# A hybrid decoder step on one core: the prompt's attention issued by head pair instead of by head group

## The chip, the core and the metric

The kernel runs on one core of a Trainium2 chip. A core has TensorE (PE, with its weight loads shown apart as PEld), VectorE (DVE), ScalarE (ACT), GpSimd (POOL) and SyncE (SP, which here only issues DMAs). Each takes its instructions in the order in which they are written; semaphores tie the engines together. The metric is the device time of one execution in microseconds, as the median of the runs shown.

## What is computed

The reference is one inference step of a two-layer model for a prompt of 1024 tokens and 8 sample sequences of 4 tokens. Layer one joins native sparse attention (8 query heads, 2 key heads, head size 64) with a gated MLP, layer two is a gated linear recurrence. The change touches the prompt's attention alone. For each block of 128 queries it has three branches, each a softmax with its own keys, merged by gates:

```python
p_c = jax.nn.softmax(jnp.where(ok_c, s_c, NEG), axis=-1) * ok_c
o_c = jnp.einsum('bghtn,bngd->btghd', p_c.astype(vc.dtype), vc)
...
p_s = jax.nn.softmax(s_s.reshape(B, NSA_KV_HEADS, HPG, Tb, n_key), axis=-1)
o_s = jnp.einsum('bghtk,bgtkd->btghd', p_s.astype(v_s.dtype), ...)
...
p_w = jax.nn.softmax(jnp.where(ok_w, s_w, NEG), axis=-1)
o_w = jnp.einsum('bghtk,bkgd->btghd', p_w.astype(vw.dtype), vw)
...
o = (g[:, :, 0] * oc + g[:, :, 1] * osl + g[:, :, 2] * ow)
y_nsa = o * jax.nn.silu(z_nsa)
```

Branch c attends to compressed blocks of 64 keys, s to selected blocks (with 16 blocks of 64 in the prompt all that lie behind the query are selected), w to a sliding window of 512. Everything is float32.

## The kernel before

The prompt has eight tiles of 128 queries. In tile i the compressed branch has 2i + 2 columns for all heads at once; the selected branch has (i + 1) x 128 key columns; the window branch as many, at most 640. A head pair c (0 to 3) is the heads c and c + 4, one of each key head. So a tile has nine "pairs": one c, four s, four w (PAIRS). A group is the four s pairs or the four w pairs of a tile (GROUPS), a unit a chunk of at most 512 score columns of one pair (UNITS).

One pair goes through five steps. PE multiplies queries and keys into a PSUM bank pair (scores; line 1192 is the helper of all matmuls). DVE adds the position bias, writes the sum to the buffer `probs` and keeps the row's minimum (L1758). ACT takes the exponential in place and the row sum (L1051). POOL takes the reciprocal of the sum with a power (L942) and multiplies sum and gate into the probabilities, in place, one instruction a head (L948). PE then turns each 128 x 128 block of probabilities (a flip, line 1196) into a PSUM bank, ACT (L1059) or DVE (L1774) copies the bank to the buffer `pT`, and PE multiplies with the values into bank 7, where the 4 x 128 columns are the four pairs and the two halves of the partitions the two key heads. At a tile's end DVE multiplies bank 7 by the gate path (`y`, L1778). The c pair has its own small form (L930 to L938 on POOL, `c_turn`, `c_values`).

`attention_steps` writes down one order of steps; PE and DVE each walk through it, ACT through the order that `act_order` makes of it, POOL through PAIRS. A step of kind `turn` (j, b, g) is for key block b of group j and key head g: four flips, one of each pair, fill one bank. It waits for the scaling of the group's last pair:

```python
pe.wait_ge(norm_done, last_pair(j) + 1)
```

The `values` step of a key block has two instructions of 512 columns, one for each key head, all four pairs side by side, in the two column halves of the array. Key head 0 is copied by ACT, key head 1 by DVE. The next group's scores are spread over the key blocks of the present one, so scores are one group ahead, and `probs` has one set for s and one for w. Three banks (4, 5, 6) take turned blocks, `pT` has two buffers. SP starts the sample sequences' cache loads for its first half when the selected group of tile 7 has been turned, those of the second half (twelve transfers of 256 KB each time) when the last y is done.

Of the kernel before, what the change touches and what calls it, by code (L numbers as in the profile page):

```python
# [23 lines left out]
P = 128  # L24
# [88 lines left out]
GROUPS = [(kind, i) for i in range(PT) for kind in "sw"]  # L113
# [3 lines left out]
LAST_UNIT = [max(n for n, u in enumerate(UNITS) if u[0] == e) for e in range(len(PAIRS))]  # L117


def last_pair(j):  # L120

    return 9 * (j // 2) + 4 * (j % 2) + 4


def blocks(j):
    return key_cols(*GROUPS[j])[0] // P


FEW = 2


def attention_steps():

    steps = []
    issued = 0

# [9 lines left out]
    def group_end(j):  # L146
        return LAST_UNIT[last_pair(j)] + 1

    score(group_end(0))
    late = None  # L150

    def values():
        j, b = late
        steps.append(("values", late))
        if GROUPS[j][0] == "w" and b == blocks(j) - 1:
            steps.append(("y", GROUPS[j][1]))

    for j, (kind, i) in enumerate(GROUPS):
        nk = blocks(j)
        ahead = group_end(j + 1) if j + 1 < len(GROUPS) else issued  # L160
        if kind == "s":
            steps.append(("c_turn", i))
        for b in range(nk):
            steps.append(("turn", (j, b, 0)))
            if late and b == 0 and kind == "s":
                values()
                late = None
            steps.append(("turn", (j, b, 1)))
            left = ahead - issued
            score(issued + -(-left // max(1, nk - 1 - b)) if left > 0 else issued)  # L170
            if b == nk - 1 and j + 2 < len(GROUPS) and blocks(j + 1) <= FEW:
                score(group_end(j + 2))
            if kind == "s" and b == 0:
                steps.append(("c_values", i))
            if late:
                values()
            late = (j, b)
    values()
    return steps


def act_order(steps):

    order, pending = [], []
    for x in steps:
        if x[0] == "scores":
            pending.append(x)
            continue
        need = -1
        if x[0] == "turn":  # L190
            need = LAST_UNIT[last_pair(x[1][0])]
        elif x[0] == "c_turn":
            need = LAST_UNIT[9 * x[1]]
        while pending and pending[0][1] <= need:
            order.append(pending.pop(0))
        order.append(x)
        if x[0] == "turn":
            order += pending
            pending = []
    return order + pending  # L200


def bank_uses(steps):

    return {x: k for k, x in enumerate(x for x in steps if x[0] in ("c_turn", "turn"))}

# [15 lines left out]
def build(nc, ins, outs):  # L222
    ctx = ExitStack()
    with ctx:
# [66 lines left out]
        probs = {"s": view(region_w, 8448, HEADS, SEQ), "w": view(region_w, 16640, HEADS, WCOLS)}  # L291
        bias_far = view(region_w, 21760, HEADS, P)
        pT = [view(region_w, 22784 + 1024 * j, KVH, 512) for j in range(2)]
# [248 lines left out]
        bank_use = bank_uses(steps)  # L542

        block_order = [x[1][:2] for x in steps if x[0] == "turn" and x[1][2] == 0]
        nth_block = {x: f for f, x in enumerate(block_order)}
        dve_uses = [x for x in steps if x[0] == "c_turn" or x[0] == "turn" and x[1][2] == 1]
        nth_dve = {x: n for n, x in enumerate(dve_uses)}
        by_bank = list(bank_use)

        def bank_is_free(eng, k):  # L550

            if k >= 3:
                x = by_bank[k - 3]
                if x in nth_dve:
                    eng.wait_ge(dve_turned, nth_dve[x] + 1)
# [1490 lines left out]
```

## Time and profile before

| | us |
|---|---|
| median of 3 runs (lowest, highest) | 1247.98 (1246.66, 1253.84) |
| the profiled execution | 1246.11 |
| its span, first to last instruction | 1244.3 |
| PE busy in the span | 1101.1 (88%) |
| DVE busy | 508.3 (41%) |
| ACT busy | 369.7 (30%) |
| POOL busy | 291.7 (23%) |

The prompt's attention begins at about 395 us, after the input projections, and its last y ends at 734.9; the sample sequences, the output projection and the second layer follow. Busy time of matmuls is modelled, since they are pipelined: prices are better read as the distance from one row's start to the next row's start. PE's clock is granted at one of two levels, 1.2 and 2.4 GHz, shown as 0.50 and 1.00.

### The profile page before, as it was taken

Reading aid. Unit: us, or ns where it says so; the run is one execution under the profiler, and the core shown is the slowest. Engines: PE = TensorE matmul, PEld = TensorE weight load, DVE = VectorE, ACT = ScalarE, POOL = GpSimd, SP = SyncE. Lnnn points to the kernel's source line nnn. Section 1 sums busy time; section 2 is a strip of 40 time slices with the busy share of each in tenths; the row PEclk is TensorE's granted clock in tenths of the full one; section 3 lists DMA queues with packets and bytes.
Section 4 is the critical chain, followed back from the end, with each engine's and each line's share of the span. In section 5 each row is a group of like instructions: output and inputs, shape, how many; then the busy total and the mean of one; then the engine's idle time right before and its main releaser. Section 6 shows DMA issues by size and latency. Waiting matters only on the chain.

```text
span 1244.3 us, 14223 instructions
## 1 busy us (share of the span) xinstructions
PE 1101.1 (88%) x5553; PEld 822.5 (66%) x5553; DVE 508.3 (41%) x1048; ACT 369.7 (30%) x632; POOL 291.7 (23%) x395
## 2 busy tenths in 40 slices
PE   5999999999997675877888876899999999998997
PEld 3555547999997343434444444688688888997884
DVE  1222213111232343454555523544469996315222
ACT  1011103111111333344354410322237777114111
POOL 1223317320001656355354400000101221000110
PEclk9999999999998677788898886799999999998999
DMA  9110034232103100000000056222231110601221
GB/s 311 35 43 26 16 75 115 75 92 51 41 11 96 41 1 1 1 1 1 1 1 1 1 177 162 83 87 89 68 90 35 34 35 18 203 1 56 68 102 59
DMA packets 70448, 74.69 MB, mean 60 GB/s; under 512 B 21730, under 2 KB 55570, under 8 KB 70383
## 3 DMA queue, kind: packets, MB, share of 16 engines
q1 hardware_dynamic: 65260, 69.15, 17.8%
q0 software_dynamic: 2496, 3.04, 0.8%
q10 hardware_dynamic: 2626, 1.62, 0.5%
q8 instruction: 44, 0.72, 0.2%
q14 instruction: 22, 0.17, 0.0%
HBM read 62.16 MB, written 16.34 MB: 63 GB/s over the span
## 4 chain that ended last, share of the span: by engine, by line
PE 81%; POOL 6%; ACT 4%; DVE 2%; issue 2%; DMA 2%; SPq 1%; ACTq 0%; POOLq 0%; DVEq 0%
PE ps L1192 74%; PE ps L1196 7%; POOL region_w L948 4%; POOL inv L942 2%; ACT region_w L1051 1%; DMA region_y<-in_w_in_a 1%; ACT L1135 1%; ACT region_w L1135 1%; ACT region_w L1059 1%; DMA region_w<-in_cache_win 1%; POOL inv L930 1%; DVE region_w L1758 0%; DMA region_w<-rel_rows_dram 0%; SPq L722 0%; SPq L724 0%
## 5 line engine op out<-in xcount | busy, mean ns | idle before, releaser
L1196 PE MATMUL ps<-ident,region_w 128*128 128x128 f32 (+2 forms) x738 | 116.6, 305 | 87.4 <-POOL region_w L948 66.6
L1196 PEld LDWEIGHTS ps<-ident,region_w 128*128 128x128 f32 (+2 forms) x738 | 92.1, 156 | 153.2 <-issue 114.4
L1192 PE MATMUL ps<-h1T_hi,w_c_hl 128*128 128x352 f32 x768 | 151.1, 326 | 12.9 <-ACT region_w L1135 8.7
L1192 PE MATMUL ps<-hT_hi,w_fm_hl 128*128 128x352 f32 x768 | 146.5, 324 | 2.8 <-DVE w_fm_hl L1629 2.8
L1192 PEld LDWEIGHTS ps<-h1T_hi,w_c_hl 128*128 128x128 f32 x768 | 129.0, 190 | 17.7 <-ACT region_w L1135 13.1
L1192 PEld LDWEIGHTS ps<-hT_hi,w_fm_hl 128*128 128x128 f32 x768 | 127.7, 188 | 3.0 <-DVE w_fm_hl L1629 2.9
L829 POOL TENSOR_SCALAR ms<-ss 128x1 f32<-128x1 f32 (+1 forms) x27 | 12.6, 468 | 386.4 <-ACT region_w L1185 177.3
L1192 PE MATMUL ps<-region_y,region_w 128*128 128x512 f32 (+3 forms) x288 | 100.4, 507 | 0.0
L948 POOL TENSOR_SCALAR region_w<-region_w,inv,gates 128x640 f32<-128x640 f32 (+7 forms) x128 | 98.7, 781 | 6.7
L1192 PE MATMUL ps<-region_w 128*128 128x512 f32 (+4 forms) x308 | 98.9, 514 | 1.4 <-DVE region_w L1816 1.4
L1059 ACT COPY region_w<-ps 128x512 f32<-128x512 f32 x66 | 38.6, 585 | 199.0 <-PE ps L1196 199.0
L1051 ACT ACTIVATE region_w<-region_w,negm 128x640 f32<-128x640 f32 (+7 forms) x128 | 92.6, 727 | 2.6 <-DVE negm L1758 2.5
L1192 PE MATMUL ps<-region_q 64*128 64x512 f32 (+3 forms) x384 | 87.6, 571 | 5.9 <-DVE negm L1758 2.4
L1192 PE MATMUL ps<-h1T_lo,w_c_hl 128*128 128x352 f32 x384 | 85.9, 325 | 0.0
L1192 PE MATMUL ps<-w_outa_hi,ya_hl 128*128 128x512 f32 (+1 forms) x288 | 81.3, 400 | 4.6 <-DVE w_outa_lo L1872 4.6
L1192 PE MATMUL ps<-hT_lo,w_fm_hl 128*128 128x352 f32 x384 | 82.7, 323 | 0.0
L1192 PEld LDWEIGHTS ps<-region_y,region_w 128*128 128x128 f32 (+1 forms) x288 | 52.8, 186 | 44.5 <-issue 37.5
L1192 PE MATMUL ps<-region_w,region_q 128*64 128x512 f32 x264 | 81.1, 698 | 1.2 <-DVE region_w L1774 1.2
L1192 PEld LDWEIGHTS ps<-region_w 128*128 128x128 f32 (+2 forms) x308 | 47.6, 181 | 43.6 <-issue 32.2
L1774 DVE COPY region_w<-ps 128x512 f32<-128x512 f32 x66 | 45.5, 690 | 73.2 <-PE ps L1196 72.8
L942 POOL TENSOR_TENSOR inv<-sums,minus_one 128x2 f32<-128x2 f32 x64 | 45.2, 706 | 95.0 <-ACT region_w L1051 95.0
L1192 PEld LDWEIGHTS ps<-h1T_lo,w_c_hl 128*128 128x128 f32 x384 | 66.1, 189 | 0.0
(243 smaller groups left out, 1488.5 us busy)
## 6 DMA issues: line engine op xcount, KB each, us to landing
region_w<-in_x_prompt SPq DMA_DIRECT2D x16, 512.0 KB, 3.5
region_w<-in_w_in_c SPq DMA_DIRECT2D x16, 512.0 KB, 3.9
rel_rows_dram<-rel_once_dram SPq DMA_DIRECT2D x8, 576.0 KB, 5.5
region_w<-in_w_in_a SPq DMA_DIRECT2D x16, 256.0 KB, 3.6
region_w<-in_w_in_a SPq DMA_DIRECT2D x8, 512.0 KB, 3.7
region_w<-in_cache_nsa SPq DMA_DIRECT2D x16, 256.0 KB, 3.0
x_dram<-region_w SPq DMA_DIRECT2D x8, 512.0 KB, 2.6
region_w<-in_w_out_c SPq DMA_DIRECT2D x2, 2048.0 KB, 9.9
```

What stands on the lines that cost most here:

```text
L829: pool.tensor_scalar(ms[0:r, norm, i:i + 1], ss[0:r, norm, i:i + 1], 1.0 / D, EPS, ALU.mult, ALU.add).then_inc(pool_chain, 1)
L930: pool.tensor_tensor(inv[:, 0, :], sums[:, i % 2, 0, :], minus_one[:, 0:HEADS], ALU.pow).then_inc(pool_chain, 1)
L942: pool.tensor_tensor(inv[:, b, c::HPG], sums[:, i % 2, b, c::HPG], minus_one[:, 0:KVH], ALU.pow).then_inc(pool_chain, 1)
L948: m = pool.tensor_scalar(x, x, inv[:, b, h:h + 1], gates[:, i, b * HEADS + h:b * HEADS + h + 1], ALU.mult, ALU.mult)
L1051: m = nc.scalar.activation(buf, buf, ACT.Exp, bias=negm[:, at:at + 1], scale=-1.0, accum_out=sums[:, i % 2, b, h:h + 1])
L1059: nc.scalar.copy(pT[f % 2][:, 0, :], ps[:, 4 + k % 3, :]).then_inc(act_turned, 1)
L1135: nc.scalar.activation(r_buf.rearrange("p (a b) -> p a b", a=3), bank3(n), ACT.Sigmoid, bias=vecT[:, VEC["b_rg_a"] + c:VEC["b_rg_a"] + c + ...
L1192: return nc.tensor.matmul(out, l, r, start=start, stop=stop, skip_group_check=True)
L1196: return nc.tensor.transpose(out, x, ident[0:k, 0:k])
L1774: v.tensor_copy(pT[f % 2][:, 1, :], ps[:, 4 + k % 3, :]).then_inc(dve_turned, 1)
```

## The change

The order is written by head pair. A `turn` step is now (e, b): pair e, key blocks b and b + 1 (one if there is no second), both key heads: four or two flips in one bank. It waits for that pair's scaling alone. Its `values` step has, for each of the blocks and key heads, an instruction of 128 columns, and stands behind the second turn that follows (one is kept back in `late` when the next is issued). Scores run up to five pairs ahead (`ahead`). The probabilities lie in six buffers of one pair each, taken in rotation (`probs_slot`); DVE waits, before it writes a buffer, for the last turn of the pair that had it. `pT` has four buffers of two blocks. A turn of even index b / 2 is copied by ACT, the others by DVE. The first instruction that clears bank 7 is now a selected one; the wait for the tile before's y stands there; `c_values` comes later, in the stream. Line numbers after the attention's helpers move up by some lines: flips are L1185, matmuls L1181, ACT's copies L1047, DVE's L1772.

```diff
+P_RING = 6
+PT_RING = 4
+TURN_BANKS = 3
...
+def probs_slot(e):
+
+    return (e - e // 9 - 1 + 2) % P_RING
...
+    def ahead(e):
+        return LAST_UNIT[min(e + P_RING - 1, len(PAIRS) - 1)] + 1
+
+    score(ahead(0))
+    for e, (kind, i, c) in enumerate(PAIRS):
+        if kind == "c":
+            continue
+        firsts = list(range(0, blocks(e), 2))
+        for at, b in enumerate(firsts):
+            steps.append(("turn", (e, b)))
+            left = max(0, ahead(e) - issued)
+            score(issued + -(-left // (len(firsts) - at)))
+            values(1)
+            late.append(("values", (e, b)))
+        if kind == "s" and c == 1:
             steps.append(("c_turn", i))
...
+            values(1)
+            late.append(("c_values", i))
+    values(0)
     return steps
+
+
+def on_act(x):
+
+    return x[0] == "turn" and x[1][1] // 2 % 2 == 0
...
-                    sp.wait_ge(turned, bank_use["turn", (len(GROUPS) - 2, PT - 1, 1)] + 1)
+                    sp.wait_ge(turned, last_turn[len(PAIRS) - 1 - HPG] + 1)
...
-                    pe.wait_ge(norm_done, last_pair(j) + 1)
-                    for c in range(HPG):
-                        m = flip(ps[:, 4 + k % 3, c * P:(c + 1) * P],
-                                 probs[kind][:, g * HPG + c, b * P:(b + 1) * P])
+                    e, b = n
+                    pe.wait_ge(norm_done, e + 1)
+                    for j in range(min(2, blocks(e) - b)):
+                        for g in range(KVH):
+                            m = flip(ps[:, 4 + k % TURN_BANKS, (2 * j + g) * P:(2 * j + g + 1) * P],
+                                     probs[probs_slot(e)][:, g, (b + j) * P:(b + j + 1) * P])
                     m.then_inc(turned, 1)
...
-                    for g in range(KVH):
-                        gp = slice(g * HD, (g + 1) * HD)
-                        m = mm(ps[gp, 7, :], (v_s if kind == "s" else v_w)[:, first // P + b, gp],
-                               pT[f % 2][:, g, :], False, kind == "w" and b == blocks(j) - 1)
+                    turn_out(pe, k)
+                    if kind == "s" and c == 0 and b == 0 and i >= 1:
+                        pe.wait_ge(y_nsa, i)
+                    for j in range(min(2, blocks(e) - b)):
+                        for g in range(KVH):
+                            gp = slice(g * HD, (g + 1) * HD)
+                            m = mm(ps[gp, 7, c * P:(c + 1) * P],
+                                   (v_s if kind == "s" else v_w)[:, first // P + b + j, gp],
+                                   pT[k % PT_RING][:, j, g, :], kind == "s" and c == 0 and b + j == 0,
+                                   kind == "w" and c == HPG - 1 and b + j == blocks(e) - 1)
                     m.then_inc(values_done, 1)
...
+                    was = [x for x in last_turn if x < e and probs_slot(x) == probs_slot(e)]
+                    if a == 0 and was:
+                        dve.wait_ge(turned, last_turn[max(was)] + 1)
```

PE before, from the end of tile 6's window group into tile 7's selected group. Flips read `ident,region_w`, values write `64x512`, scores are the `region_q` rows, `ident,lc` and `vc_bd` belong to the compressed branch.

```order
L1192 MATMUL ps<-region_w,region_q 64x512 x2
L1196 MATMUL ps<-ident,region_w 128x128 x8
L1192 MATMUL ps<-region_w,region_q 64x512 x2
L1196 MATMUL ps<-ident,lc 128x128
L1196 MATMUL ps<-ident,region_w 128x128 x4
L1192 MATMUL ps<-region_w,region_q 64x512 x2
L1196 MATMUL ps<-ident,region_w 128x128 x4
L1192 MATMUL ps<-region_q 128x128 x2
L1192 MATMUL ps<-region_q 128x512 x2
L1192 MATMUL ps<-region_w,vc_bd 128x128 x4
L1196 MATMUL ps<-ident,region_w 128x128 x8
```

The four flips behind `ident,lc` wait for the whole selected group's scaling; all its scores stand ahead of these rows. PE after, at the same place: the first row is the values of tile 6's last window turn, the flips are all of tile 7's first selected pairs:

```order
L1181 MATMUL ps<-region_w,region_q 64x128 x2
L1185 MATMUL ps<-ident,region_w 128x128 x4
L1181 MATMUL ps<-region_q 128x128 x2
L1181 MATMUL ps<-region_w,region_q 64x128 x4
L1185 MATMUL ps<-ident,region_w 128x128 x4
L1181 MATMUL ps<-region_q 128x512 x2
L1181 MATMUL ps<-region_w,region_q 64x128 x4
L1185 MATMUL ps<-ident,region_w 128x128 x4
L1181 MATMUL ps<-region_q 128x128 x2
L1181 MATMUL ps<-region_w,region_q 64x128 x4
```

Flips, scores and values now alternate in short runs, and the stream has no step at which a whole group is waited for.

ACT before, over the scores of tile 7's selected pairs (1024 columns; two instructions a pair), which it takes while tile 6's window group is turned:

```order
L1044 ACTIVATE lc<-lc 128x128
L1051 ACTIVATE region_w,sums<-region_w,negm 128x1024 x2
L1059 COPY region_w<-ps 128x512
L1051 ACTIVATE region_w,sums<-region_w,negm 128x1024 x2
L1059 COPY region_w<-ps 128x512
L1051 ACTIVATE region_w,sums<-region_w,negm 128x1024 x2
```

ACT after, over the same scores:

```order
L1032 ACTIVATE lc<-lc 128x128
L1047 COPY region_w<-ps 128x512 x2
L1047 COPY region_w<-ps 128x256
L1039 ACTIVATE region_w,sums<-region_w,negm 128x1024 x2
L1047 COPY region_w<-ps 128x512
L1047 COPY region_w<-ps 128x256
L1039 ACTIVATE region_w,sums<-region_w,negm 128x1024 x2
```

A pair's exponentials now stand behind both of ACT's copies of the pair that is being turned; before, one copy of each key block stood between them. POOL's and SP's instructions stand in the same order as before.

## Rows read from the trace of the kernel before

**Rows 1.** Stretch: us; busy PE, PEld, DVE, ACT, POOL; PEclk, DMA share, GB/s.

```profile
395.00:735.00 340.00, 263.58 (x1313) 136.60 (x1313) 158.44 (x529) 132.34 (x330) 159.93 (x216) 0.82 0.07 22
```

**Rows 2.** Waits from 395 to 735: engine, line, waited for; us, times, longest.

```profile
POOL inv L942 <- ACT region_w L1051: 95.0, 29, 10.8
...
PE ps L1196 <- POOL region_w L948: 66.6, 14, 7.1
```

**Rows 3.** PE over time at a group's end: start, us, what, idle before.

```profile
692.55 1.09 PE L1196 MATMUL ps<-ident,region_w 128*128 128x128 f32 x4 [4.59 <-POOL region_w L948]
693.57 1.98 PE L1192 MATMUL ps<-region_w,region_q 128*64 128x512 f32 x4
695.47 1.12 PE L1196 MATMUL ps<-ident,region_w 128*128 128x128 f32 x4
```

**Rows 4.** PE over time inside a window group of tile 6.

```profile
642.85 0.66 PE L1196 MATMUL ps<-ident,region_w 128*128 128x128 f32 x4
643.44 1.35 PE L1192 MATMUL ps<-region_q 64*128 64x128 f32 x8
644.72 1.16 PE L1192 MATMUL ps<-region_w,vc_bd 128*128 128x128 f32 x8
645.71 1.04 PE L1196 MATMUL ps<-ident,region_w 128*128 128x128 f32 x8
...
652.45 1.13 PE L1192 MATMUL ps<-region_q 64*128 64x512 f32 x4
653.51 1.08 PE L1192 MATMUL ps<-region_w,region_q 128*64 128x512 f32 x4
654.52 1.09 PE L1196 MATMUL ps<-ident,region_w 128*128 128x128 f32 x8
655.54 0.49 PE L1192 MATMUL ps<-region_q 64*128 64x128 f32 x4
655.96 1.08 PE L1192 MATMUL ps<-region_w,region_q 128*64 128x512 f32 x4
```

**Rows 5.** Weight loads over time, of c_values and of 512-column values.

```profile
595.65 0.97 PEld L1192 LDWEIGHTS ps<-region_w,vc_bd 128*128 128x128 f32 x8 [0.95 <-issue]
...
598.90 0.20 PEld L1192 LDWEIGHTS ps<-region_w,region_q 128*64 128x64 f32 x4 [0.76 <-issue]
```

**Rows 6.** POOL: two pairs of tile 0 over time; groups by line (busy, mean ns).

```profile
403.93 0.71 POOL L942 TENSOR_TENSOR inv<-sums,minus_one 128x2 f32<-128x2 f32 x1
405.58 0.71 POOL L942 TENSOR_TENSOR inv<-sums,minus_one 128x2 f32<-128x2 f32 x1
L948 POOL TENSOR_SCALAR region_w<-region_w,inv,gates 128x640 f32<-128x640 f32 x40 | 34.6, 874 | 2.1
L930 POOL TENSOR_TENSOR inv<-sums,minus_one 128x8 f32<-128x8 f32 x8 | 13.2, 1651 | 74.6 <-DVE sums L1763 74.6
```

**Rows 7.** Busy time by stretch, for the granted clock (PEclk, after the busy times).

```profile
409.00:421.00 12.00, 11.63 (x54) 8.49 (x55) 4.81 (x29) 3.77 (x17) 6.23 (x12) 0.50 0.01 2
421.00:428.00 7.00, 5.12 (x33) 2.56 (x32) 5.03 (x26) 4.65 (x18) 4.62 (x8) 1.00 0.00 1
725.00:735.00 10.00, 9.21 (x55) 4.48 (x53) 3.46 (x5) 2.34 (x4) 0.00 (x0) 1.00 0.61 192
```

**Rows 8.** Groups by line: copies and exponentials; busy, mean ns; idle before, releaser.

```profile
L1774 DVE COPY region_w<-ps 128x512 f32<-128x512 f32 x66 | 45.5, 690 | 73.2 <-PE ps L1196 72.8
L1059 ACT COPY region_w<-ps 128x512 f32<-128x512 f32 x66 | 38.6, 585 | 199.0 <-PE ps L1196 199.0
L1051 ACT ACTIVATE region_w<-region_w,negm 128x640 f32<-128x640 f32 x40 | 32.8, 822 | 0.8 <-DVE negm L1758 0.8
```

**Rows 9.** SP's sample loads and PE's first use of the second half.

```profile
718.00 8.50 SPq L724 DMA_DIRECT2D region_w<-in_cache_nsa  x8
735.64 8.00 SPq L724 DMA_DIRECT2D region_w<-in_cache_nsa  x8
752.61 1.97 PE L1196 MATMUL ps<-ident,region_w 128*128 128x128 f32 x8 [8.38 <-DMA region_w<-in_cache_win]
```

More of the change, by code:

```diff
@@ L135, in attention_steps @@
     issued = 0
+    late = []
     def score(upto):
@@ L144, in score, with values @@
         issued = max(issued, upto)
[L146 to L161, printed above, removed]
-            steps.append(("c_turn", i))
[L163 to L178, printed above, removed]
-    return steps
+    def values(keep):
+        while len(late) > keep:
+            x = late.pop(0)
+            steps.append(x)
+            if x[0] == "values":
+                e, b = x[1]
+                if PAIRS[e][0] == "w" and PAIRS[e][2] == HPG - 1 and b + 2 >= blocks(e):
+                    steps.append(("y", PAIRS[e][1]))
+    def ahead(e):
[12 more added lines that the diff above has]
+        if kind == "s" and c == 1:
+            steps.append(("c_turn", i))
+            values(1)
+            late.append(("c_values", i))
+    values(0)
+    return steps
+def on_act(x):
+    return x[0] == "turn" and x[1][1] // 2 % 2 == 0
 def act_order(steps):
@@ L188, in act_order @@
             continue
[L189 to L193, printed above, removed]
+        if x[0] not in ("turn", "c_turn"):
+            continue
+        need = LAST_UNIT[x[1][0] if x[0] == "turn" else 9 * x[1]]
         while pending and pending[0][1] <= need:
             order.append(pending.pop(0))
[L196 to L199, printed above, removed]
+        if on_act(x):
+            order.append(x)
+        order += pending
+        pending = []
     return order + pending
-def bank_uses(steps):
-    return {x: k for k, x in enumerate(x for x in steps if x[0] in ("c_turn", "turn"))}
 FM_A = ([("z", j, "act") for j in range(4)]
@@ L289, in build @@
         bias = view(region_w, 0, HEADS, SEQ)
-        probs = {"s": view(region_w, 8448, HEADS, SEQ), "w": view(region_w, 16640, HEADS, WCOLS)}
+        probs = [view(region_w, 8448 + KVH * SEQ * j, KVH, SEQ) for j in range(P_RING)]
         bias_far = view(region_w, 21760, HEADS, P)
-        pT = [view(region_w, 22784 + 1024 * j, KVH, 512) for j in range(2)]
+        pT = [view(region_w, 22784 + 512 * j, 2, KVH, P) for j in range(PT_RING)]
         probT_c = view(region_w, 24832, P)
@@ L541, in build, with turn_out @@
         steps = attention_steps()
[L542 to L555, printed above, removed]
-                else:
-                    eng.wait_ge(act_turned, nth_block[x[1][:2]] + 1)
+        turns = [x for x in steps if x[0] in ("turn", "c_turn")]
+        nth_turn = {x: k for k, x in enumerate(turns)}
+        last_turn = {x[1][0]: k for k, x in enumerate(turns) if x[0] == "turn"}
+        act_count = [sum(on_act(y) for y in turns[:k + 1]) for k in range(len(turns))]
+        def turn_out(eng, k):
+            if on_act(turns[k]):
+                eng.wait_ge(act_turned, act_count[k])
+            else:
+                eng.wait_ge(dve_turned, k + 1 - act_count[k])
         def spread(ap, n, axis=2):
@@ L1321, in _ @@
             for what, n in steps:
-                k = bank_use.get((what, n))
-                if k is not None:
-                    bank_is_free(pe, k)
+                k = nth_turn.get((what, n))
+                if k is not None and k >= TURN_BANKS:
+                    turn_out(pe, k - TURN_BANKS)
                 if what == "scores":
```

73 lines of the change are left out of this document (35 added, 38 removed).

## The prediction

> **What bounds the kernel now.** I read the busy time by stretch first. The prompt's attention runs from 395 to 735 us, 340 us, and in it TensorE (PE) is busy 264 us at a mean granted clock of 0.82, GpSimd (POOL) 160, VectorE (DVE) 158, ScalarE (ACT) 132 [rows 1]. So PE is the nearest bound, and still it idles 76 us and runs part of the rest at the lower clock. The waits say why: 66.6 us of PE's idle time, in 14 waits, ends with POOL's scaling of probabilities (L948), and POOL itself idles 95.0 us behind ACT's exponentials [rows 2]. A group is four head pairs, and PE turns nothing of a group before POOL has scaled its last pair, while scores run only one group ahead. So at each group's end the last chunk of scores goes through DVE, ACT and POOL with PE idle. The row at 692.55 is such a place: PE waited 4.59 us for L948 [rows 3]. The first work after it is slow: 512-column values (four records) took 1.90 us from 693.57 to 695.47 [rows 3], and 1.01 from 653.51 to 654.52 [rows 4].
>
> **PE's prices at the full clock**, from start to next start [rows 4]: a run of 4 flips 0.59 (642.85 to 643.44), of 8 flips 1.02 (654.52 to 655.54), so 0.11 a flip and 0.37 for 2. Scores: a 512-column unit 1.06 (from 652.45), a 128-column unit alone 0.42 (from 655.54), one of each in one run 1.28 (from 643.44). So 128 more columns in a run cost 0.22, and what is left of the lone unit, 0.20, is the price of changing over to scores. A 512 unit then streams 0.86, and on that line 256 columns stream 0.43 and 384 0.65. Values of 512 columns cost 1.01, that is 0.86 and a change of 0.15.
>
> **Before, by these prices.** 66 key blocks x (1.02 + 1.01) = 134. Score units (44 of 512, 12 of 384, 12 of 256, 28 of 128) stream 37.8 + 7.8 + 5.2 + 6.2 = 57, and 49 runs x 0.20 = 10. The compressed branch I take as 2.2 a tile in both kernels (0.99 of it from 644.72 to 645.71 [rows 4]), 18. Sum 218. The other 122 us of the stage are waits and the lower clock. That is what there is to win.
>
> **The change part by part.**
> Flips: 528 in both, but now in 152 runs (112 of 4, 40 of 2): 112 x 0.59 + 40 x 0.37 = 81, where 66 x 1.02 = 67 stood.
> Values: 66 pairs of 512-column instructions become 264 pairs of 128-column ones. The trace before has none of that shape. Below, a pair can't cost less than a quarter of the old stream, 0.22; above, it could cost what a lone 128-column score pair does, 0.42. I take 0.22 and one change of 0.15 a run, 0.59 for two blocks and 0.37 for one, since the nearest row, c_values (four 128-column instructions, eight records), takes 0.99 in all. So 112 x 0.59 + 40 x 0.37 = 81, where 67 stood; at 0.42 for each pair it would be 111, 30 more.
> Scores: the same 57, but 89 runs, so 18 of changes and not 10. The compressed branch stays 18. Sum 81 + 81 + 75 + 18 = 255: **PE gets 37 us more of its own work.**
> What goes is the group's end. A pair is turned as soon as its own scaling is done, and scores run five pairs ahead. POOL's pair takes 1.65 us at 128 columns (403.93 to 405.58) and, with 0.87 for each of its two L948 rows at 640, 2.5 [rows 6]. PE needs for such a pair 2 x (0.59 + 0.59) + 2 x 0.37 + 0.42 + 1.06 = 4.6. So POOL is hidden from the third tile on, by 2 us a pair. In tiles 0 and 1 POOL sets the pace: 8 x 1.65 + 8 x 1.86 (256 columns, on the line) + 2 x 2.35 for the compressed pairs (1.65 of it L930 [rows 6]) = 33, where PE's own is 28 (pairs of 0.37 + 0.37 + 0.42 = 1.16 and 0.59 + 0.59 + 0.63 = 1.81): +5. Before the first pair is scaled (404) PE can only score: of these 9 us about 3.5 are used, for one compressed pair and five of 0.4 to 0.5, so +5.5.
> Evictions: 132 of 512 columns become 152 of 512 or 256. ACT takes 96 (38.6 us of busy time become about 50), DVE 56 (45.5 become about 34). So ACT's work in the stage becomes about 143, DVE's 147, POOL's stays 160 [rows 1], all well under PE's 255: they lie beside it. In a 640-column pair ACT has 2 x 0.82 + 0.585 + at most 0.585 = 2.8 us [rows 8] of PE's 4.6. A run's eviction begins about 0.7 us after the run's start and takes 0.6 to 0.7, so the values could start 1.5 us after it. In the order they stand behind the second run that follows, with two other runs of values between: 5 x 0.59 = 3 us or more. That covers an exponential pair of ACT (1.7) that the copy has to wait for, nearly. I book +3 for what is missed, with 0 and 45 as ends.
> Waits: that for y moves to the first values of a tile; behind it on PE stand the next flips, and for those wait ACT and DVE. DVE reaches y up to one unit of logits late (two passes of 512 columns, by the copy's 0.69 [rows 8] 1.4) and takes about 0.7, PE has 0.6 to 1.6 of other work: 0 to 2 us at seven tiles, +5. DVE's new wait for a buffer is for the pair six before, whose last turn stands ahead of these scores on PE: 0.
> SP's wait for the last group's turns becomes one for the last selected pair: same place. POOL's order is unchanged.
>
> **The clock.** The row 409 to 421 shows 0.50 with PE busy 11.63 of 12 us; from 421 it is 1.00 [rows 7]. The new kernel starts at the lower level too. Its first tile is sparse, and twice as dear it is still near POOL's pace; tile 1 at that level would add (1.8 x 1.81 - 1.86) x 8 = 11 us. I book +8, ends 0 and 20. Later no wait of several us is left.
>
> **Sum.** 255 + 5.5 + 5 + 8 + 5 + 3 = 281.5, and about 1 for the last y, against the stage's 340: -57.5. The tail: the sample's first twelve transfers, issued at 718.00, were due after 17 us as the second twelve were (735.64 to 752.61 [rows 9]), just as the last window group ended. Now four window pairs without scores follow the issue, 4 x 3.1 = 12.4 and y, about 14: up to 3 us of these transfers stick out and push the second twelve, +1.5. Together -56. The profiled execution's 1246.11 us (span 1244.3) become 1190; the median of the runs is 1.9 higher, so **1192 us**.
>
> **Rivals.**
> *Evictions come late* (0.3 us at each of 152 runs, three banks and four buffers not being enough): 46 in place of 3, 1235. For it: ACT takes its order as it stands, and a copy can stand behind an exponential pair that waits for DVE. Against: ACT and DVE idle 200 and 73 us at these copies for want of work [rows 8].
> *Weight loads stand in front of the short matmuls.* Four loads of 64 columns show 0.20 [rows 5]; 264 such sets in full are 53, about 45 over what the changes hold: 1237. Against: in c_values eight loads of 128 columns are busy 0.97 us [rows 5] of the 0.99 that the eight matmuls take, so they overlap. The Trainium skill, "TensorE: Matmul & The Clock Gate", Part 3, "What overlaps and what doesn't", says that weight loads overlap matmuls in flight only where the row group differs, which is not so here. With its load of P/1.2 ns, 53 ns for 64 columns, 528 loads would be 28 us, an estimate from that page, and the sum 1220; the c_values row speaks against it.
> *PE stays at the lower clock* (slower). Values cost 1.90 and 4 flips 1.02 there (692.55 to 693.57 [rows 3]), about 1.8 times as much. All 255 us so would be 204 more, less the 8 booked: 1388. The change loses once about 80 us of PE's work, a third, runs at that level (64 / 0.8). For it: runs get shorter, with more changes between. Against: from 725 to 735, where flips and values alternate with waits for evictions, the clock is 1.00 [rows 7]. The Trainium skill, same page, Part 4 (PE-mode transpose), says that the full rate does not engage for transposes; by that rule, with a third of PE's work in flips, this rival would be likelier. The row last named, half flips, speaks against it.
> *The run-ahead doesn't reach over a tile's start*: the compressed pair, its reciprocal of 1.65 us and y hold PE there as the groups' ends did, 8 x 3.5 = 28: 1220.
>
> **Chances.** Forecast with its own range 1174 to 1215: 0.72. Late evictions 0.10, loads 0.06, tile starts 0.05, lower clock 0.07. Low end: nothing for the clock, y, late evictions and the tail, -73.5 us and so 1174. High end: loads, 1237. A measurement here tells 0.5% (6 us) from no change. Faster: 0.72 + 0.05 and nearly all of the 0.16, 0.90; same 0.03; slower 0.07.
>
> **What would show it.** Right: no wait of PE for L948 over 2 us after 440; granted clock 1.00 from about 440 to the stage's end; flips and values about 81 us each at full clock, c_values' pace in the values; PE busy over 90% from tile 2 on; the stage's end near 680. Wrong: waits of PE for the copies (L1047, L1772) that sum to tens of us; values pairs at 0.4; 0.5 in the clock row past 450; idle PE at each tile's start behind y.

## The result and the profile after

The changed kernel takes 1185.09 us (median of 4 runs, 1181.83 to 1187.05) where the kernel before, run beside it, takes 1250.91 (4 runs): a ratio of 0.947, with an interval of 0.943 to 0.952. Forecast were 1192 (1174 to 1237). The profiled execution takes 1187.05 us (span 1185.2), 59.1 less than the one of before; the medians are 65.8 apart, since the profiled execution is the longest of the four here, and the one before was shorter than the four it is measured against. Three stretches account for the 59.1:

| us | before | after | difference |
|---|---|---|---|
| attention, from 395 to the end of the last y | 339.9 | 275.5 | -64.4 |
| sample stage, from there to the output projection's first matmul | 52.2 | 58.0 | +5.8 |
| the rest behind it | 459.0 | 458.5 | -0.5 |

So the attention gave 7 us more than forecast (282.5 us, the prediction's 281.5 and 1 for the last y), and in this execution the stage behind it took nearly 6 back.

Busy time of the changed kernel by stretch (us; PE, PEld, DVE, ACT, POOL; granted clock; DMA share; GB/s), to be read against [rows 1]:

```profile
395.00:671.00 276.00, 260.36 (x2104) 159.45 (x2104) 148.54 (x520) 143.86 (x360) 161.08 (x216) 0.96 0.09 28
430.00:672.00 242.00, 235.80 (x1972) 143.44 (x1971) 137.30 (x450) 129.61 (x301) 138.66 (x177) 1.00 0.05 14
476.00:670.00 194.00, 191.96 (x1626) 117.50 (x1625) 112.72 (x365) 99.04 (x215) 102.64 (x122) 1.00 0.06 16
```

PE is busy almost as long as before, though it now does more work, because hardly any of that work runs at 0.50. From the fourth tile on (third line) it is busy 99% of the time.

Its waits from 395 to 671 (us, times, longest), against [rows 2]:

```profile
POOL inv L929 <- ACT region_w L1039: 53.6, 30, 4.8
...
PEld ps L1181 <- ACT region_w L1047: 17.9, 27, 1.0
...
PE ps L1185 <- POOL region_w L936: 8.6, 4, 2.9
...
PE ps L1181 <- DVE region_y L1777: 2.6, 3, 0.9
```

The 66.6 us behind POOL are 8.6, and all but 1.2 of these lie before 430. No wait of PE's matmuls ends with a copy: the 17.9 us stand at the weight loads (PEld), which run ahead of the matmuls. PE in tile 5, as [rows 4] showed tile 6, then a tile's start with its wait for y, then the weight loads of the first rows:

```profile
560.56 0.66 PE L1185 MATMUL ps<-ident,region_w 128*128 128x128 f32 x4
561.15 0.66 PE L1181 MATMUL ps<-region_w,region_q 128*64 128x128 f32 x8
561.74 0.66 PE L1185 MATMUL ps<-ident,region_w 128*128 128x128 f32 x4
...
587.30 0.49 PE L1181 MATMUL ps<-region_q 64*128 64x128 f32 x4
588.64 0.66 PE L1181 MATMUL ps<-region_w,region_q 128*64 128x128 f32 x8 [0.85 <-DVE region_y L1777]
```

```profile
560.56 0.42 PEld L1185 LDWEIGHTS ps<-ident,region_w 128*128 128x128 f32 x4 [0.17 <-issue]
561.15 0.42 PEld L1181 LDWEIGHTS ps<-region_w,region_q 128*64 128x64 f32 x8 [0.17 <-issue]
```

From start to start four flips cost 0.59 us and the values of two blocks 0.59, the two prices of the forecast to the digit. The eight loads of a values run (two records for each instruction) are busy 0.42 us inside these 0.59.

And the stage behind the attention, against [rows 9]: SP's sample loads, PE's first work on each half, the first matmul of the output projection, and a stretch of that stage.

```profile
657.03 8.51 SPq L711 DMA_DIRECT2D region_w<-in_cache_nsa  x8
...
671.22 8.70 SPq L711 DMA_DIRECT2D region_w<-in_cache_nsa  x8
```

```profile
672.41 3.56 PE L1185 MATMUL ps<-ident,region_w 128*128 128x128 f32 x16 [2.66 <-DMA region_w<-in_cache_win]
...
687.68 1.97 PE L1185 MATMUL ps<-ident,region_w 128*128 128x128 f32 x8 [5.01 <-DMA region_w<-in_cache_win]
...
694.79 6.83 PE L1181 MATMUL ps<-avg,region_w 128*128 128x2 f32 x32
...
728.50 1.19 PE L1181 MATMUL ps<-w_outa_hi,ya_hl 128*128 128x512 f32 x2 [4.58 <-DVE w_outa_lo L1871]
```

```profile
679.00:734.00 55.00, 38.65 (x213) 28.88 (x214) 22.96 (x81) 11.96 (x22) 0.00 (x0) 0.50 0.47 135
...
691.00:711.00 20.00, 20.00 (x123) 15.69 (x122) 5.83 (x27) 1.44 (x6) 0.00 (x0) 0.50 0.52 149
```

The second half's first flips come 17.2 us behind the last y (17.7 before), so the transfers are not later. From there to the output projection are 40.8 us, and 34.5 before. The clock is 0.50 from 679 to 734 without a break, where the kernel before had two stretches at 1.00 (10.2 us together).

### The profile page after: what moved, and what is told of

It reads as the page before. It is cut to its first block, busy times and chain, and to the rows that moved or that the text cites. A ratio compares the mean times of both kernels' runs of the same rounds, so it can differ in the third digit from the quotient of the medians.

```text
span 1185.2 us, 15810 instructions
## 1 busy us (share of the span) xinstructions
PE 1106.7 (93%) x6345; PEld 854.2 (72%) x6345; DVE 497.2 (42%) x1038; ACT 381.2 (32%) x662; POOL 287.5 (24%) x395
## 4 chain that ended last, share of the span: by engine, by line
PE 88%; ACT 3%; DVE 2%; DMA 2%; issue 2%; POOL 1%; SPq 1%; ACTq 0%; DVEq 0%; POOLq 0%
PE ps L1181 79%; PE ps L1185 9%; DMA region_y<-in_w_in_a 1%; ACT L1124 1%; ACT region_w L1124 1%; DMA region_w<-in_cache_win 1%; POOL inv L917 0%; POOL region_w L936 0%; DVE region_w L1754 0%; SPq L711 0%; DMA region_w<-rel_rows_dram 0%; SPq L709 0%; ACT region_w L1114 0%; ACT w_c_hl L1067 0%; POOL inv L929 0%
## 5 line engine op out<-in xcount | busy, mean ns | idle before, releaser
L1181 PE MATMUL ps<-h1T_hi,w_c_hl 128*128 128x352 f32 x768 | 151.2, 326 | 12.8 <-ACT region_w L1124 8.7
L1185 PE MATMUL ps<-ident,region_w 128*128 128x128 f32 (+2 forms) x738 | 128.7, 301 | 27.9 <-POOL region_w L936 8.6
L1181 PE MATMUL ps<-hT_hi,w_fm_hl 128*128 128x352 f32 x768 | 147.7, 326 | 2.8 <-DVE w_fm_hl L1622 2.8
L1181 PEld LDWEIGHTS ps<-h1T_hi,w_c_hl 128*128 128x128 f32 x768 | 129.0, 190 | 17.7 <-ACT region_w L1124 13.1
L1185 PEld LDWEIGHTS ps<-ident,region_w 128*128 128x128 f32 (+2 forms) x738 | 86.4, 151 | 62.0 <-issue 31.3
L1181 PEld LDWEIGHTS ps<-hT_hi,w_fm_hl 128*128 128x128 f32 x768 | 128.9, 190 | 3.0 <-DVE w_fm_hl L1622 2.9
L1181 PE MATMUL ps<-region_w 128*128 128x512 f32 (+4 forms) x308 | 98.9, 514 | 1.4 <-DVE region_w L1815 1.4
L1181 PE MATMUL ps<-region_y,region_w 128*128 128x512 f32 (+3 forms) x288 | 99.1, 503 | 0.0
L1181 PEld LDWEIGHTS ps<-region_w,region_q 128*64 128x64 f32 x1056 | 55.1, 137 | 57.0 <-issue 32.4
L1181 PE MATMUL ps<-region_w,region_q 128*64 128x128 f32 x1056 | 91.8, 289 | 2.7 <-DVE region_y L1777 2.6
L1754 DVE CUSTOM_DVE_ANT_0 region_w<-ps,region_w 128x128 f32<-128x128 f32 (+3 forms) x128 | 57.7, 488 | 77.0 <-PE ps L1181 76.7
L1181 PE MATMUL ps<-region_q 64*128 64x512 f32 (+3 forms) x384 | 84.9, 526 | 2.1 <-DVE lc L1735 1.9
L1181 PE MATMUL ps<-h1T_lo,w_c_hl 128*128 128x352 f32 x384 | 85.8, 325 | 0.0
L1181 PE MATMUL ps<-w_outa_hi,ya_hl 128*128 128x512 f32 (+1 forms) x288 | 81.0, 399 | 4.6 <-DVE w_outa_lo L1871 4.6
L1181 PEld LDWEIGHTS ps<-region_y,region_w 128*128 128x128 f32 (+1 forms) x288 | 52.3, 184 | 43.8 <-issue 36.8
L1047 ACT COPY region_w<-ps 128x512 f32<-128x512 f32 (+1 forms) x96 | 49.7, 518 | 105.6 <-PE ps L1185 105.4
L1181 PE MATMUL ps<-hT_lo,w_fm_hl 128*128 128x352 f32 x384 | 83.1, 325 | 0.0
L1181 PEld LDWEIGHTS ps<-region_w 128*128 128x128 f32 (+2 forms) x308 | 47.6, 181 | 43.6 <-issue 32.2
L1181 PEld LDWEIGHTS ps<-h1T_lo,w_c_hl 128*128 128x128 f32 x384 | 66.2, 189 | 0.0
```

What stands on the lines that cost most here:

```text
L1047: nc.scalar.copy(pT[k % PT_RING][:, 0:w, :, :].rearrange("p b g t -> p (b g t)"), ps[:, 4 + k % TURN_BANKS, 0:w * KVH * P]).then_inc(act_t ...
L1181: return nc.tensor.matmul(out, l, r, start=start, stop=stop, skip_group_check=True)
L1185: return nc.tensor.transpose(out, x, ident[0:k, 0:k])
L1754: x = v.tensor_tensor_reduce(probs[probs_slot(e)][:, g, a:b], ps[:, slot + g, 0:b - a], table, 1.0, least, ALU.add, ALU.min, to)
```

## The experiments

Theory: in the kernel before, PE waited at each group's end for the chain through DVE, ACT and POOL, and ran slowly behind the wait; the wait for one pair and the scores five pairs ahead remove both, for about 37 us of added work at known prices. Rivals: only the finer wait or only the run-ahead matters; copies come late; a change between runs costs other than reckoned; the clock is a consequence that costs nothing by itself. Medians stand beside those of the kernel before on the same chip (1247 to 1253), and the ratio is to these. In profiled executions the attention's first matmul lies between 395 and 399, so stages are compared from there.

### The whole group is waited for again

```diff
-        need = LAST_UNIT[x[1][0] if x[0] == "turn" else 9 * x[1]]
+        need = LAST_UNIT[x[1][0] + HPG - 1 - PAIRS[x[1][0]][2] if x[0] == "turn" else 9 * x[1]]
...
-                    pe.wait_ge(norm_done, e + 1)
+                    pe.wait_ge(norm_done, e + HPG - PAIRS[e][2])
```

> The changed kernel with one part undone: a turn waits again until the last pair of its group of four is scaled, and ACT takes the group's exponentials ahead of the group's first copy; the six buffers, the scores five pairs ahead, the 128-column values and the turns of two blocks stay. Theory (the grain of the wait and the run-ahead work together): for a selected group the scores of the fourth pair are issued only in the last turns of the tile before, so PE waits 4 to 6 us for POOL's scaling at each of 7 tile starts and 0 to 2 us at the window groups, and the granted clock falls again after some of these waits: +45 us (30 to 60), 1230 us. Rival A (the run-ahead alone hides the chain, the grain of the wait is nothing): +0 to 10 us, at most 1195. Rival B (the grain is all): as the kernel before, near 1250.

Measured: 1245.04 us, 0.999 (0.997 to 1.001). All of the gain is gone with one wait (and ACT's order that goes with it), though the ring of six buffers, the run-ahead and the short values stay. Waits of the stage, and PE at a tile's start:

```profile
PE ps L1185 <- POOL region_w L936: 50.3, 11, 7.8
```

```profile
458.41 0.66 PE L1181 MATMUL ps<-region_w,region_q 128*64 128x128 f32 x8
466.51 1.09 PE L1185 MATMUL ps<-ident,region_w 128*128 128x128 f32 x4 [7.44 <-POOL region_w L936]
```

The clock's mean over the stage falls from 0.96 to 0.87. Rival A is out. The theory's size was too low (+45, at most +60, where the medians give +60 and the ratios +64), and by its time alone this run fits rival B, the grain is all, as well. The next two runs decide that: there the fine wait stays. The 37 us of added work stay in here too, so the run doesn't say that the run-ahead is worth nothing by itself.

### Scores two and three pairs ahead

```diff
-P_RING = 6
+P_RING = 3
...
```

With four buffers it is `P_RING = 4`.

> The changed kernel with three buffers of probabilities in place of six, so scores run two pairs ahead and not five (the compressed sums stand one unit earlier on DVE, so that the order has no cycle); the wait for one pair alone stays. Theory (the chain through DVE, ACT and POOL takes 6 to 7 us for a pair of 512 columns or more, and the run-ahead hides it): a pair's scores now stand one pair of PE's work (4 to 6 us) ahead, or none for the first two selected pairs of a tile, so PE waits for POOL 1 to 2 us at most pairs and about 5 us at two pairs of each tile, with the lower clock behind them: +100 us (60 to 140), about 1285, slower than the kernel before. Rival (the finer wait is the gain, the ring only needs to be there): +0 to 15 us, at most 1200.

> The changed kernel with four buffers of probabilities, scores three pairs ahead in place of five. Theory (the chain needs 6 to 7 us, two pairs of PE's work are 8 to 12 in the later tiles; only the third selected pair of a tile, whose scores are held up by the compressed pair's place in the count, has one pair of work): waits of 2 to 3 us at 7 tile starts and about 10 us more in the first three tiles: +25 us (10 to 40), about 1210. Rival (three ahead are enough): within 5 us. Rival (the dependence on the ring is steep, as from two to five): over +50.

Measured: 1283.32 us with three buffers, 1.030 (1.028 to 1.031), and 1213.79 with four, 0.974 (0.970 to 0.977). PE's waits for POOL with three:

```profile
PE ps L1185 <- POOL region_w L936: 74.1, 32, 6.0
```

and with four:

```profile
PE ps L1185 <- POOL region_w L936: 28.1, 13, 5.2
```

With five, three and two pairs of run-ahead PE waits 8.6, 28.1 and 74.1 us for POOL. The sizes are the theory's (1285 and 1210 were expected). With two pairs, less than the one group (four pairs) of the kernel before, the fine wait is slower than that kernel; with three it brings about half of the gain. So rival B is out: the fine wait needs the run-ahead. Not run was the other way round, the old order with its long values and waits for a group, but with scores more than one group ahead; whether that would do as well is open.

### Values one turn earlier

```diff
-            values(1)
+            values(0)
```

> The changed kernel with values one turn earlier: none is kept back, each run of values stands behind the first turn that follows its own. From a turn's start to its values are then three runs of 0.59 us, 1.8 us, and a copy ends about 1.4 us after its turn's start, later where ACT is in a pair of exponentials (1.7 us). Theory (copies are on time with two turns between, and only just with one): +10 us (0 to 20) in waits of PE for the copies of L1047. Rival (late evictions were already there in the changed kernel, hidden in the rows as a slower pace): +25 to 45 us. Rival (the holding back does nothing): within 3 us.

Measured: 1188.62 us, 0.953 (0.951 to 0.954), an interval that overlaps the changed kernel's; the stage is 280 us in place of 276. One wait of PE ends with a copy:

```profile
PE ps L1181 <- DVE region_w L1772: 2.1, 1, 2.1
```

The rest is a lower mean clock in the stage (0.94 for 0.96), so the copies were on time but for one, and the turn held back is worth some 4 us in this execution. The rival of late evictions is out.

### Turns of one key block

```diff
-        firsts = list(range(0, blocks(e), 2))
+        firsts = list(range(0, blocks(e), 1))
...
```

The widths of flips, copies and values follow, and ACT and DVE still copy by turns.

> The changed kernel with turns of one key block: 264 runs of 2 flips and 264 runs of 2 values instructions in place of 152 runs each; columns, ring and waits stay. Theory (prices: a change over to another kind of run costs 0.15 us on top of 0.11 a flip and 0.22 a pair of 128-column values): flips 264 x 0.37 = 98 in place of 81, values 98 in place of 81, a few more changes to scores: +35 us (30 to 42), about 1220, with PE busy all the same. Rival (a change costs nothing, a run's cost is in its columns): +0 to 5 us. Rival (the fixed part of 264 copies makes evictions late): +50 us or more, in waits of PE for L1047 and the DVE copies.

Measured: 1226.23 us, 0.984 (0.982 to 0.986), so +41. PE inside tile 4:

```profile
560.10 0.44 PE L1185 MATMUL ps<-ident,region_w 128*128 128x128 f32 x2
560.47 0.44 PE L1181 MATMUL ps<-region_w,region_q 128*64 128x128 f32 x4
560.84 0.44 PE L1185 MATMUL ps<-ident,region_w 128*128 128x128 f32 x2
```

A run costs 0.37 us, as reckoned. PE's busy time in the stage is 299 us (260 in the changed kernel), and another 4 us are waits for y (6.7 in place of 2.6). So short runs have their price, and evictions are not it: PE's waits for copies are 1.2 us in all.

### The clock without the order

In the kernel before, idle matmuls stand in front of each group's first turn:

```diff
+                    if b == 0 and g == 0:
+                        for _ in range(8):
+                            mm(ps[:, 4 + k % 3, :], ident[:, :], qT[:, 0, 0:512], True, True)
                     pe.wait_ge(norm_done, last_pair(j) + 1)
```

> The kernel before, with eight idle matmuls of 512 columns (nothing reads them; 3.4 us at the full clock) in front of the first turn of each group, where PE waits 3.5 to 7.1 us for POOL. It parts the two things that went away together with the change: waiting, and the lower clock behind the waits. Theory (both cost by themselves): the granted clock stays at 1.00 between the group ends, the 36 us that the lower clock costs there (90 us at that level in the kernel before, 18 in the changed one, half of the difference) come back in part, since faster scores reach DVE earlier: -20 us (-10 to -36), about 1227. Rival A (the chain through DVE, ACT and POOL sets the group ends, a faster PE only waits longer): within 5 us of the kernel before. Rival B (the idle matmuls run at the lower clock and hold the flips up): slower by 10 us or more.

Measured: 1265.84 us, 1.013 (1.010 to 1.017), slower, as rival B had it but for another reason: the clock was up, but the eight (two records each) took twice the time reckoned and held the flips up. So on the question this run says only that the clock can be held. The stage, and a group's end in it:

```profile
398.00:751.00 353.00, 338.62 (x1568) 165.30 (x1568) 158.73 (x530) 132.28 (x330) 160.52 (x216) 0.98 0.07 22
```

```profile
623.06 7.13 PE L1192 MATMUL ps<-region_q,ident 128*128 128x512 f32 x16
630.03 1.04 PE L1196 MATMUL ps<-ident,region_w 128*128 128x128 f32 x8
```

With four in place of eight:

> The kernel before with four idle matmuls of 512 columns in front of each group's first turn in place of eight. With eight, each took 0.87 us and not the 0.43 that was reckoned, 7.0 us a group, longer than most waits, though the clock stayed at 1.00 but for 14 us. Four are 3.5 us and lie inside the waits of 3.5 to 7.1 us. Theory (the lower clock costs by itself: 90 us of the stage at 0.50 are 45 us of PE's work done twice as slowly): the clock stays at 1.00 for most of the stage, the waits stay as long as they are: -30 us (-15 to -40), about 1217. Rival A (the chain sets the groups' ends, a faster PE waits longer): within 5 us of the kernel before. Rival B (3.5 us are too few to keep the clock up): within 5 us too, with 0.50 in the clock row behind the waits.

Measured: 1222.13 us, 0.975 (0.972 to 0.978). The stage, and a group's end in it:

```profile
398.00:714.00 316.00, 289.70 (x1447) 141.37 (x1448) 158.68 (x530) 132.26 (x330) 160.51 (x216) 0.97 0.08 24
```

```profile
669.64 3.60 PE L1192 MATMUL ps<-region_q,ident 128*128 128x512 f32 x8
674.32 0.66 PE L1196 MATMUL ps<-ident,region_w 128*128 128x128 f32 x4 [1.08 <-POOL region_w L948]
```

The waits are still there, filled: idle matmuls and the wait behind them sum to 4.7 us here, where [rows 3] has 4.59. With the clock at 0.97 instead of 0.82 the stage is 26 us shorter and the kernel 2.5%. So the lower clock behind the waits was a cost of its own, by the ratios nearly half of what the change gained (0.025 of 0.053), and the old order could have had that part. Rival A is out.

### The stage behind the attention

Sample loads cut up on SP (first half's windows at the attention's start, its pages in two parts, the second half's windows behind the first window pair):

```diff
+            load_wins(0)
...
+            sp.wait_ge(turned, last_turn[last_s - 1] + 1)
+            load_pages(0, range(HALF))
+            sp.wait_ge(turned, last_turn[last_s] + 1)
+            load_pages(0, range(HALF, 2 * HALF))
+            sp.wait_ge(turned, last_turn[last_s + 1] + 1)
+            load_wins(1)
+            sp.wait_ge(y_nsa, PT)
+            load_pages(1, range(2 * HALF))
```

> The changed kernel with the sample loads cut up on SP: the first half's window transfers at the attention's start, its first four pages behind the last turn of the third selected pair of tile 7, the other four where they were, the second half's window transfers behind the first window pair, and only its pages behind the last y. Theory (after the last y PE waits 1.9 and 5.0 us for these transfers): the first wait goes and the second half lands after 8 issues, about 5 us earlier: -6 us (-4 to -10), about 1179. Rival (the transfers are not what sets the end there, the clock is): within 2 us.

Idle matmuls in PE's waits instead (`keep(n)` issues n of them; one of the places):

```diff
             def turn_pages(f, bank, h):
+                keep(6 if f else 3, True)
                 pe.wait_ge(samp_in[f], 16 * (2 * HALF + HALF))
```

> The changed kernel with idle matmuls (nothing reads them) in PE's waits of the sample stage: 3 of 512 columns before the first half's flips, 6 before the second half's, and 6, 3, 3 (before the last result) or 12 of 224 columns in three later waits; of the later ones only those before the flips of probabilities, the values and the output projection are there. Theory (the 5 us that the change gave back behind the last y are the lower clock, 0.50 from 679 to 734 without a break): part of the stage is granted 1.00, -5 us (-2 to -12), about 1180. Rival (the clock there does not matter, engines wait for one another): within 2 us. Rival (it stays at 0.50 and the idle matmuls hold PE up): +3 to +8 us.

Measured: 1179.76 us, 0.944 (0.942 to 0.947), and 1180.12, 0.946 (0.944 to 0.948). Each interval overlaps that of the changed kernel, so the medians alone don't tell them from it. The stretch from the last y to the output projection is 49.5 and 54.7 us in place of 58.0. But in the nine kernels that leave this stage as it is (both kernels and the runs above), one execution of each, it lies between 51.4 and 58.0, so only the 49.5 stands clear. With the loads cut up:

```profile
673.29 1.97 PE L1194 MATMUL ps<-ident,region_w 128*128 128x128 f32 x16 [0.80 <-DVE region_y L1786]
...
685.04 1.97 PE L1194 MATMUL ps<-ident,region_w 128*128 128x128 f32 x8 [2.49 <-DMA region_w<-in_cache_nsa]
```

PE starts on the first half right behind y and on the second 11.8 us behind it (17.2 in the changed kernel, 15.6 to 18.3 in the nine). With idle matmuls:

```profile
670.00:725.00 55.00, 51.31 (x306) 37.98 (x307) 20.42 (x78) 8.26 (x18) 0.00 (x0) 0.75 0.56 166
```

The granted clock is 0.75 where the changed kernel had 0.54 (671 to 728), and the stretch is 3.3 us shorter, though two of the rows held PE up by 3 and 1 us; that alone lies within what an untouched stage shows. Both together, with fewer idle matmuls, and then with SP reading the page numbers ahead:

> The changed kernel with the sample loads cut up as in e6_split_loads and idle matmuls in PE's waits of the sample stage, fewer than in e7_tail_busy: none before the first half's flips, 1 of 512 columns before the means, 3 before the second half's flips, and of 224 columns 6, 3, 2 and 10 in the later waits. Theory (the late transfers and the lower clock are two losses that add): e6 gave -5 and e7 -5, in e7 two rows of idle matmuls held PE up by 3 and 1 us: together -12 us (-8 to -18), about 1173. Rival (both take the same wait away): 1179.

> As e10_both, and SP reads the second half's eight page numbers before the wait for the last y and not between its transfers. Theory (eight issues at 1.05 us each, 8.3 us, set the landing): the issues take about half of that, the transfers land 2 to 3 us earlier, and PE's last wait for them (2.5 us in e6) goes: -2 us against e10_both. Rival (the transfers themselves set the landing): within 1 us of e10_both.

Measured: 1176.07 us, 0.939 (0.936 to 0.941), and 1176.49, 0.938 (0.936 to 0.941); the stretch is 47.1 and 47.2 us. Both intervals lie below the changed kernel's and, by a hair, below that of the cut-up loads alone, so the idle matmuls do give something: the two losses add, if not fully. The page numbers ahead halve the issues (8.14 us become 4.17 on SP's queue), but in both kernels PE comes to the second half out of the idle matmuls with no wait for a transfer; whether the transfers landed earlier doesn't show, and this stays open.

### Two turns in a run

The price of a change, used the other way: two turns stand together, then their scores, then the values of the two turns before, on top of the kernel with cut-up loads and idle matmuls.

```diff
+    def flush():
+        for x, _, _ in run:
+            steps.append(x)
...
+        values(0)
+        for x, _, _ in run:
+            late.append(("values" if x[0] == "turn" else "c_values", x[1]))
+        run.clear()
```

> As e10_both, and the attention's turns go in twos: two turns (up to eight flips, two banks), then the scores of both, then the values of the two turns before; a tile's last turn stands alone where the count is odd. Runs of flips become 87 in place of 163 (the compressed turns among them), of values 83 in place of 158, of scores 71 in place of 98; columns, copies and waits stay. Theory (prices: 0.15 us for each change to flips or values, 0.20 to scores; 264 runs in place of 152 cost 41 us in e4_one_block): (76 + 75) x 0.15 + 27 x 0.20 = 28 us less of PE's work, of which a few are lost to copies that come late and to POOL's pace in the first two tiles: -20 us (-10 to -28) against e10_both, about 1156. Rival (a change costs only where a run is two flips long; longer runs gain nothing more): within 4 us of e10_both. Rival (two banks a run leave one for the next, PE waits for copies): no gain or slower, with waits of flips for L1047 and the DVE copies.

Measured: 1160.04 us, 0.928 (0.925 to 0.931): the fastest of all, 13 us below the kernel with both edits by the ratios (0.0105 of 1248), in the lower half of what was expected. The stage, and PE inside it:

```profile
398.00:656.00 258.00, 239.25 (x2104) 164.27 (x2104) 150.91 (x520) 142.94 (x360) 161.30 (x216) 0.94 0.11 34
```

```profile
559.81 1.09 PE L1204 MATMUL ps<-region_w,region_q 128*64 128x128 f32 x16
560.83 1.09 PE L1208 MATMUL ps<-ident,region_w 128*128 128x128 f32 x8
561.86 1.77 PE L1204 MATMUL ps<-region_q 64*128 64x512 f32 x8
```

A run of eight flips or sixteen values records costs 1.02 to 1.03, two runs cost 1.18. PE's busy time falls by 21 us, the stage by 17: in the first two tiles a run now waits for two pairs' scaling (11.5 us of waits for POOL, 8.6 before), and one more wait of 2.6 us, for DVE, has come in.

## Why the prediction was right, and where it was not

**PE's own work: right.** 255 us at the full clock were forecast. The rows of the stage, from start to next start and without idle time, sum to 260: flips 81, values 82, scores 79, the compressed branch 19, before rounding. About 18 of these lie at the lower clock, half of which is its cost; so some 251 are own work. Values at a quarter of the old stream plus 0.15 a run were the unseen price; they came out at 0.59 a run, and the upper bound of 0.42 a pair was 30 us off. That c_values was the row to go by is confirmed.

**The waits: right.** After 430 PE waits 1.2 us for POOL. The time before the first pair is scaled and POOL's pace in the first two tiles, 10.5 us forecast, are 9.5 us of idle time before 430. The lower clock was booked with 8 and cost 9. The waits for y, 5 us, were 2.6 in 3 tiles. Late evictions, 3 us with 45 as an end, were 0, and the run without the held-back turn, with 2.1 us of such waits, says that the cover is wide. These small terms, with own work a little below, are the 7 us by which the attention beat its forecast.

**The weight loads: the rival is out.** By the Trainium skill, "TensorE: Matmul & The Clock Gate", Part 3, "What overlaps and what doesn't", loads in the same row group would not overlap matmuls in flight; this case shows otherwise. The 1056 records of these loads are busy 55 us and add nothing: in the run of two turns eight more loads and matmuls cost 1.02 less 0.59, 0.43 us, no more than two quarters of the old stream of 0.86. The prediction counted 528 loads; each instruction has two records, so its estimate of 28 us would have been 56.

**The lower clock: the rival is out for the attention.** The clock is 1.00 from 430 to 672 with flips a third of PE's work. The same page of the Trainium skill, Part 4 (PE-mode transpose), has it that the full rate does not engage for transposes; this case shows otherwise.

**The rival of the run-ahead at a tile's start: out.** The longest wait for y there is 0.95 us. The run with the whole-group wait shows what it would have been: 7.44.

**The tail: wrong.** The step was "up to 3 us of these transfers stick out and push the second twelve, +1.5". The transfers do stick out (2.66 us), but the second twelve hang on the last y and come as before. What the step left out is the clock: I looked at the granted clock in the attention alone and took the rest as a block that only moves. From the second half's flips to the output projection the same instructions stand in all nine kernels that leave this stage as it is. Busy times and clock there: the kernel before, the changed one, the one with four buffers, the one before with eight idle matmuls, the one with the whole-group wait, the one with turns of one block.

```profile
752.60:787.10 34.50, 23.85 (x190) 17.03 (x191) 15.42 (x70) 6.44 (x16) 0.00 (x0) 0.65 0.50 149
...
687.70:728.50 40.80, 30.88 (x191) 22.96 (x191) 15.51 (x70) 6.46 (x16) 0.00 (x0) 0.50 0.45 129
...
717.00:751.60 34.60, 23.92 (x190) 17.11 (x191) 15.44 (x70) 6.46 (x16) 0.00 (x0) 0.65 0.52 153
...
766.70:807.50 40.80, 30.88 (x191) 22.95 (x191) 15.56 (x70) 6.49 (x16) 0.00 (x0) 0.50 0.47 134
...
749.40:785.40 36.00, 25.46 (x191) 18.05 (x191) 15.46 (x70) 6.50 (x16) 0.00 (x0) 0.59 0.52 153
...
731.00:768.80 37.80, 27.84 (x191) 19.92 (x191) 15.53 (x70) 6.48 (x16) 0.00 (x0) 0.55 0.44 131
```

DVE's and ACT's work is the same in all, PE's grows as the clock falls, and the stretch grows with it. The other three fit: 40.8 us at 0.50 twice, 37.8 at 0.55. So the clock is the cause of the 6.3 us. The new order is not shown to be: the changed kernel with four buffers has the short stretch, the old order with idle matmuls the long one, and there is one profiled execution of each. What decides when the clock rises there, the runs don't show.

**The number: partly luck.** The profiled execution is 3 us under its forecast of 1190, 7 from the attention less 4 from the stage behind it. The median is 7 us under its own, because it was put 1.9 us above the profiled execution and came out 2.0 below; nothing in the argument stands behind that part.

## What to carry to other kernels

Where an engine waits for a chain of others, the grain of the wait and the run-ahead are one measure: the wait for a single pair with scores two pairs ahead was slower than the start, and five pairs ahead with a wait for the group, with the short runs' added work, brought nothing. A wait of several us costs PE twice, by itself and by the lower clock behind it, and the second part can be bought back with idle matmuls that are shorter than the wait (-2.5% here) and is lost again with ones that are longer (+1.3%). When a tuned stage has become bound by PE's own work, count the changes between kinds of runs: at 0.15 to 0.20 us each they were the next 13 us.

## What the runs showed of the hardware

A 512-column float32 matmul that fills all 128 rows takes 0.87 us at the full clock (7.0 for eight), as long as the two 64-row ones of a score unit together (0.86 [rows 4]). The two key heads' instructions run side by side (in the trace of the kernel before the records of the two heads at 652.45 start within 0.01 us of each other), and I had reckoned an idle matmul as half of such a unit, so they took twice as long.

From 691 to 711 of the changed kernel PE was busy 20.00 of 20 us by the profile, and the granted clock was 0.50 all the time; the longest piece of it are the 32 matmuls of two columns at 694.79 (6.83 us; the same 32 took 3.73 at 1.00, from 675.70 with the loads cut up). In the attention it was 1.00 for 242 us. I had taken it that a busy PE gets its clock back. That waits lower the clock shows in the kernel before (0.82 in the stage, 0.97 with the waits filled); the Trainium skill, "TensorE: Matmul & The Clock Gate", Part 1, "HAM oscillation — how this bites in real kernels", tells the same of waits for transfers.
